# The first tile's expert rows finished inside the second tail, and VectorE's routing cut into six pieces

## What is computed

```
q = (h @ w_q).reshape(B, S, PEER_HEADS, 2, PEER_HALF)
s1, s2 = q against the two sets of 128 sub-keys
v1, i1 = top_k(s1, 16); v2, i2 = top_k(s2, 16)          # routing
top, ci = top_k(v1[:, None] + v2[None, :], 16)
expert = i1[ci // 16] * 128 + i2[ci % 16]; gate = softmax(top)
act = gelu(h . expert_down[expert]) * gate
y   = sum over the 128 experts of act * expert_up[expert]
```

## Time and profile before

| | |
|---|---|
| median of 3 runs| 4313.49 us (4313.34 to 4319.21)|
| the profiled execution| 4317.19 us, span 4315.4 us|
| PE busy| 2814.7 us (65%)|
| DVE busy| 2301.3 us (53%)|
| POOL busy| 1443.1 us (33%)|
| ACT busy| 541.6 us (13%)|
| data moved| 1413.21 MB|

### The profile page before, as it was taken

How to read it: one execution, slowest core, us unless ns; L and a number is a source line. 1 busy time by engine, 2 the same in 40 slices (tenths; PEclk the granted TensorE clock), 3 DMA queues, 4 the chain that set the end, 5 groups by cost and what they waited for, 6 DMA issues and landing times.

```text
span 4315.4 us, 37435 instructions
## 1 busy us (share of the span) xinstructions
PE 2814.7 (65%) x15012; PEld 1619.7 (38%) x15012; DVE 2301.3 (53%) x3585; ACT 541.6 (13%) x1191; POOL 1443.1 (33%) x1109
## 2 busy tenths in 40 slices
PE   3797899977899999997893334434344334434435
PEld 2686787877875555453451101101001001101101
DVE  7397697652176233325465555664555664444442
ACT  2211211210110000111111101100001001000000
POOL 2321212000003223233233356454356454354352
PEclk9898999988999999998995555555555555555555
DMA  7544424488658889889688899999999999999998
GB/s 287 183 173 149 139 99 163 171 328 316 201 198 342 305 347 367 344 336 366 253 322 335 355 404 422 412 413 422 416 399 412 412 412 422 421 422 422 421 421 370
DMA packets 303724, 1413.21 MB, mean 327 GB/s; under 512 B 24384, under 2 KB 24512, under 8 KB 167104
## 3 DMA queue, kind: packets, MB, share of 16 engines
q0 software_dynamic: 152064, 1107.36, 62.6%
q1 hardware_dynamic: 145568, 291.53, 19.4%
q10 hardware_dynamic: 5920, 11.94, 0.7%
HBM read 1403.35 MB, written 7.39 MB: 327 GB/s over the span
## 4 chain that ended last, share of the span: by engine, by line
PE 42%; DMA 37%; DVE 11%; POOL 5%; issue 4%; ACT 2%; SPq 0%; ACTq 0%; DVEq 0%; POOLq 0%
PE psum L610 42%; DMA front<-in_down,back 22%; DMA front<-in_up,back 9%; POOL front L581 4%; DVE front L1577 3%; DMA front<-in_w_in 2%; DMA back<-in_ada_w 2%; DVE back L1290 1%; DVE back L1352 1%; DMA back<-in_up,back 1%; ACT back L1116 1%; DVE back L1555 0%; POOL back L581 0%; DVE back L1512 0%; DVE back L1521 0%
## 5 line engine op out<-in xcount | busy, mean ns | idle before, releaser
L610 PE MATMUL psum<-front 128*32 128x512 f32 (+2 forms) x6608 | 1410.0, 664 | 999.2 <-DMA front<-in_up,back 851.8
L1577 DVE CUSTOM_DVE_ANT_0 front<-front,back 128x2048 f32<-128x2048 f32 x512 | 1168.7, 2291 | 1391.5 <-DMA front<-in_down,back 1274.4
L610 PEld LDWEIGHTS psum<-front 128*32 128x32 f32 (+1 forms) x6608 | 582.3, 163 | 1759.7 <-issue 1404.6
L581 POOL DMA_INDIRECT front<-in_down,back x512 | 622.1, 1215 | 930.1 <-DVE back L1577 657.6
L581 POOL DMA_INDIRECT front<-in_up,back x442 | 539.5, 1221 | 1001.1 <-PE psum L610 953.8
L610 PE MATMUL psum<-back,front 128*32 128x128 f32 (+3 forms) x4400 | 636.0, 457 | 331.9 <-DMA back<-in_up,back 164.2
L610 PEld LDWEIGHTS psum<-back,front 128*32 128x32 f32 (+1 forms) x4400 | 372.2, 168 | 603.1 <-issue 316.6
L559 POOL TENSOR_TENSOR w_low<-front,w_high 128x2048 fp32r<-128x2048 f32 x33 | 153.4, 4650 | 589.5 <-ACT w_high L1004 589.5
L610 PE MATMUL psum<-x_high,w_high 128*128 128x512 f32 x640 | 258.6, 404 | 51.1 <-issue 22.4
L610 PE MATMUL psum<-x_low,w_high 128*128 128x512 f32 x640 | 256.1, 400 | 0.0
L610 PE MATMUL psum<-x_high,w_low 128*128 128x512 f32 x640 | 255.9, 400 | 0.0
(11 more groups left out here) (160 smaller groups left out, 1700.5 us busy)
## 6 DMA issues: line engine op xcount, KB each, us to landing
front<-in_w_in SPq DMA_DIRECT2D x116, 1024.0 KB, 6.7
back<-in_ada_w SPq DMA_DIRECT2D x64, 1024.0 KB, 8.5
front<-in_ada_w POOLq DMA_DIRECT2D x32, 1024.0 KB, 8.6
front<-in_w_out SPq DMA_DIRECT2D x32, 1024.0 KB, 5.6
front<-in_w_q SPq DMA_DIRECT2D x32, 1024.0 KB, 5.4
front<-in_w_conv_o SPq DMA_DIRECT2D x16, 1024.0 KB, 6.8
front<-in_w_attn_o SPq DMA_DIRECT2D x16, 512.0 KB, 3.8
front<-in_down,back POOLq DMA_INDIRECT x512
```

Source lines behind the costliest of these rows:

```text
L581: nc.gpsimd.indirect_dma_start(out=row_, out_offset=None, in_=table[:, :], in_offset=bass.IndirectOffsetOnAxis(ap=idx4[:, t % 2, c:c + 1], ...
L610: return nc.tensor.matmul(o, a, b, start=start, stop=stop)
L1577: V.tensor_tensor_reduce(d_row[s], d_row[s], h2r, 1.0, 0.0, ALU.mult, ALU.add, pre[:, b // 16 % 2, b % 16:b % 16 + 1]).then_inc(dots_done, 1)
```

## The change

1. **Places instead of positions.** A new constant `DRAIN = 32` and `place(p)` split the walk in two. Positions 0 to 159 are the first tile alone: 128 blocks and 32 positions in which its lagging work (up rows, gelu, the last group's norm) drains. Positions from 160 on are blocks 128 to 511 as before, so block 128 begins at position 160. Everything that looks back (`b - LAG`, the unit, the group) only looks back inside its own part.
2. **A new pace.** `PACE[i] = min((i + 1) * 160 // 71, 160)`: 2.25 positions per chunk, in steps of 2, 2, 2, 3, and 160 is reached after chunk 71 (the end of the first `q` group). The chunks 72 to 83 have no retrieval work.
3. **GpSimd's order** follows: downs 0 to 127 with ups 0 to 105 in between, then ups 106 to 127 alone, then downs 128 to 149 alone, then pairs again.
4. **Routing in pieces.** `top16` is split into `first8` and `next8`, and `route(t, n)` into six steps. For tiles 2 and 3 the steps stand at every second position from 28 on, with two dot products between; `gates` moves to 20 positions after the first step, ScalarE's `gate_exp` from offset 34 to 44. In the tails all six steps still come in one go.
5. Two waits (`h2_quarter` for J = 4, `z_sum` for J = 3) name the counts that fit the new order.

```diff
-END = BLOCKS + 64
+DRAIN = 32
+END = BLOCKS + DRAIN + 64
+def place(p):
+    return (p, 0, 128) if p < 128 + DRAIN else (p - DRAIN, 128, BLOCKS)
 def block_pace():
-    at, out = 0, []
-    for i in range(tail_chunks(1)):
-        if 64 <= i < 67:
-            at += (3, 3, 2)[i - 64]
-        else:
-            at += 1 + i % 2
-        out.append(at)
-    assert at == 128, at
-    return out
+    last = 48 + 16 + TAIL[1][1] // P + 4
+    return [min((i + 1) * (128 + DRAIN) // last, 128 + DRAIN) for i in range(tail_chunks(1))]
...
-            for i in range(BLOCKS + UP_LAG):
-                if i < BLOCKS:
+            for first, last in ((0, 128), (128, BLOCKS)):
+                for i in range(first, last + UP_LAG):
+                    if i < last:
...
-                b = i - UP_LAG
-                if b >= 0:
+                    b = i - UP_LAG
+                    if b >= first:
...
                 if J >= 2 and i == 0:
-                    pe.wait_ge(out_ready, J - 1)
+                    pe.wait_ge(out_ready, J if J == 4 else J - 1)
...
-                pe.wait_ge(h2r_ready, min(4 * (J + 2), 4 * GROUPS))
+                pe.wait_ge(h2r_ready, 4 * (J + 1) if J in (3, GROUPS - 1) else 4 * (J + 2))
...
-                    p = pos_
-                    if p % 32 == 0 and p < BLOCKS:
+                    b, first, last = place(pos_)
+                    if b % 32 == 0 and b < last:
                         for i in range(4):
-                            h2_quarter(p // 32, i)
-                    if 0 <= p - LAG < BLOCKS:
-                        weighted_rows(p - LAG)
+                            h2_quarter(b // 32, i)
+                    if first <= b - LAG < last:
+                        weighted_rows(b - LAG)
...
-            def route(t, n):
+            def route(t, n, step):
...
-                    t, n = p // 128 + 1, (p % 128 - 28) // 24
-                    if 2 <= t < TT and p % 128 >= 28 and n < 4:
-                        if (p % 128 - 28) % 24 == 0:
-                            route(t, n)
-                        if (p % 128 - 28) % 24 == 12:
+                    t, n = b // 128 + 1, (b % 128 - 28) // 24
+                    if first and t < TT and b % 128 >= 28 and n < 4:
+                        step = (b % 128 - 28) % 24
+                        if step % 2 == 0 and step < 12:
+                            route(t, n, step // 2)
+                        if step == 20:
                             gates(t, n)
```

More of the change, by code:

```diff
@@ L586, in _ @@
             pool.wait_ge(ada2_used, 2 * KT)
-            for i in range(BLOCKS + UP_LAG):
-                if i < BLOCKS:
[L589 to L596, removed]
-                b = i - UP_LAG
-                if b >= 0:
[L599 to L604, removed]
+            for first, last in ((0, 128), (128, BLOCKS)):
+                for i in range(first, last + UP_LAG):
+                    if i < last:
+                        s, _, prev = D_SLOT[i]
+                        if i % 128 < 32 and i % 8 == 0:
+                            pool.wait_ge(routed, 4 * (i // 128) + i % 128 // 8 + 1)
+                        if prev is not None:
+                            pool.wait_ge(dots_done, prev + 1)
+                        if i == WIDE:
+                            pool.wait_ge(g_done, DONE[1, "sc", 3] + 4)
+                        gather(down, d_row[s], i, d_in[s])
+                    b = i - UP_LAG
+                    if b >= first:
+                        s, _, prev = U_SLOT[b]
+                        if prev is not None:
+                            pool.wait_ge(u_used, prev + 1)
+                        if b == WIDE:
+                            pool.wait_ge(g_done, DONE[1, "sc", 3] + 4)
+                        gather(up, u_row[s], b, u_in[s])
         @block.tensor
@@ L1144, in retrieve @@
                 while pos_ < upto:
[L1145 to L1155, removed]
+                    b, first, last = place(pos_)
+                    if b % 32 == 0 and b < last:
+                        h2_quarters(b // 32)
+                    unit = b // 16 - 1
+                    if first <= 16 * unit < last:
+                        if b % 16 == 3:
+                            unit_gelu(unit)
+                        if 7 <= b % 16 < 15:
+                            block_weights(16 * unit + 2 * (b % 16 - 7))
+                            block_weights(16 * unit + 2 * (b % 16 - 7) + 1)
+                    J = b // 32 - 1
+                    if first <= 32 * J < last and b % 32 == 24:
                         z_squares(J)
-                    if 0 <= J < GROUPS and p % 32 == 26:
+                    if first <= 32 * J < last and b % 32 == 26:
                         z_std(J)
-                    t, n = p // 128 + 1, (p % 128 - 34) // 24
-                    if t >= 2 and t < TT and p % 128 >= 34 and (p % 128 - 34) % 24 == 0 and n < 4:
+                    t, n = b // 128 + 1, (b % 128 - 44) // 24
+                    if first and t < TT and b % 128 >= 44 and (b % 128 - 44) % 24 == 0 and n < 4:
                         gate_exp(t, n)
@@ L1513, in top16, with next8 @@
                 st.seen(st.n)
+            def next8(vals, inds, src, count):
                 for i in range(count):
@@ L1605, in retrieve @@
                 while pos_ < upto:
[L1606 to L1608 removed]
+                    b, first, last = place(pos_)
+                    J = b // 32 - 1
+                    if first <= 32 * J < last and b % 32 == 28:
                         finish(J)
[L1610 to L1618 removed]
+                    if b < last:
+                        dot(b)
+                    unit = b // 16 - 1
+                    if b % 16 == 5 and first <= 16 * unit < last:
+                        unit_act(unit)
+                    t, n = b // 128 + 1, (b % 128 - 28) // 24
[4 more added lines that the diff above has]
+                        if step == 20:
                             gates(t, n)
@@ L1689, in tail @@
                     dve.wait_ge(act_took, ATOOK[c, "sc", i] + 4)
-                    route(c, i)
+                    for step in range(6):
+                        route(c, i, step)
                     if i:
```

76 lines of the change are left out of this document (38 added, 38 removed).

## The result

The changed kernel took 4361.27 us (median of 4, 4359.42 to 4366.44), the kernel before 4314.50 us in the same measurement: a ratio of 1.0111, 95% interval 1.0099 to 1.0124. The change costs 47 us. The forecast was 4300 us, with 4345 as the upper end of the range. The profiled span is 4357.6 us; my sum was 4302.

What follows compares the result with a forecast made beforehand. TensorE was taken to bound tail 1 and DMA the rest. 2364 + 65 + 1794 + 10 + 69 = 4302 us of span (tail +71, fewer pairs -44, routing -40, together -13), so 4300 us; range 4256 to 4345.

Steps and rivals of the forecast that it cites:

- Part 1: Beginning of tail 1: TensorE waits 21 us (17 to 24) for VectorE; the first twelve chunks end at 1386.
- Part 2: Dense stretch, chunks 13 to 57: DMA becomes the bound, 620 us; chunk 57 ends at 2007 (1965 to 2030).
- Part 3: End of tail 1: +5 us before the x chunks, -22 there, -21 in the q groups; block 128's dot at 2364.
- Part 4: After the tail, blocks 128 to 149, downs only: 22 x 2.97 = 65 us instead of 109 (2.485 to 3.46 each).
- Part 5: Routing of tile 2 onward: pieces fit into idle time, so 10 us of the 50 lost stay (3 to 50).
- The end: From the last dot to the end of the kernel: 69 us, as before.
- TensorE did not stay the bound: Rival for tail 1, chance 0.20: TensorE stays the bound, chunk 57 ends at 1965, time 4258 us.
- The clock: Rival for the dense stretch, chance 0.17: TensorE's waits put chunks at 1.2 GHz, 25.4 us each; with four, 4345 us.
- Collisions of gathers with pieces: Rival for the routing, chance 0.06: gather issues slow beside VectorE's pieces, up to 108 us, time up to 4408.
- Half the routing: Rival for the routing, chance 0.17: the pieces give back only half, since groups' beginnings empty the queue, 4320 us.

Runs made afterwards that it cites:

- e3: The changed kernel with PACE held at 13 for the first nine chunks, removing TensorE's wait at the w_attn_o product: 4354.75 us, 1.0091 of the kernel before.
- e9: The changed kernel with half of tail 1's gate products left out (less TensorE work, same loads): 4326.95 us, 1.0032 of the kernel before.
- e10: The changed kernel with only half of each gate weight chunk loaded in tail 1 (less DMA, same matmuls): 4334.05 us, 1.0051 of the kernel before.
- e6: The changed kernel without ScalarE's copy of h2r for groups 1 to 3: 4357.86 us, 1.0083 of the kernel before.
- e5: The changed kernel with five buffers from block 131 on instead of 160 (WIDE = 131): 4337.33 us, 1.0045 of the kernel before.
- e1: The kernel before with only the routing of tiles 2 and 3 in six pieces, no drain: 4290.23 us, 0.9938 of the kernel before.

## Why the prediction was wrong

The forecast was 13 us faster; the kernel is 47 slower. The forecast was a small difference of large terms, +71 against -84, and three of its terms were mis-sized in the same direction: 26 us up to block 128, 8 us in the stretch of down rows, 22 us behind it. Either of the two large ones alone turns the sign, since the forecast gain was 13 us. The order below is that of the prediction.

**Part 1 was right.** TensorE waits 23.3 us for VectorE (forecast 21, bounds 17 and 24), and the first twelve chunks end at 1383.6 (1386). e3 showed that taking the wait away brings 6.5 us and not 23: loads run during the wait, too, and would have to be made up behind it.

**Part 2 had the right mechanism and the wrong size; this is the largest step that failed.** DMA became the bound (share 0.99; e9, e10). Chunk 57 ended at 2035.3 and not at 2007, beyond my upper end of 2030. There were 258.0 MB in the stretch, 246 loads and not 242, some 10 us. Each took 2.52 us and not 2.56, which took 10 back. The rest is the 27 us of dips around the groups' beginnings. My upper end of 2030 stood for just that ("if each group's beginning, which stops the dots, also empties the queue"), and I took nothing of it into the value. The mixed stretch of 75 us in which DMA's share was 1.01 was a piece without a group's beginning, so it could not price one. Where the dips lie is shown; what makes them is open (e6).

**Part 3 was right.** From chunk 57 to the x chunks 93 us (92 to 93 by the forecast), the x stage 55.4 (77 - 22 = 55), the `q` groups 181.3 (184). The price of emptying them is what I saw and did not weigh: DMA idles at a share of 0.27 for 182 us. By DMA's price, the 22 up loads that moved are worth 22 x 2.485 = 55 us. The tail grew by 96.7, so 42 us were lost in it, where the forecast lost 16 (71 - 55).

**Part 4 was too low by 8 us:** 73.3 and not 65, 3.33 us per dot, inside the bounds of 2.485 and 3.46 and near the row from which the upper bound came. The nearest row was nearer than the middle that I took. e5 gives the cause, three buffers; with five it is 60.4, 2.74 us per dot.

**Part 5 was too low by 22 us:** 31.9 and not 10. The mechanism was right and its size half of the forecast: the pieces gave back 23 us in e1 (52.4 to 29.0) and 20.6 here, not 40. What stayed begins with the group at block 160: its dot waits 9.33 us for ScalarE as before (8.68), and some 8.5 us are lost there; I gave it 2. Some 3.5 more are lost from block 176 to 184, in the second routing, where the up blocks still have three buffers. Five buffers from block 131 on take 14.6 of the 31.9 us away, these two losses among them (e5). Some 17 us stay in every kernel with five, about 1.5 us for each of the 11 groups from block 160 to 480. The 42 us read from the slices were not all routing: slice 22 held this group too.

**The end:** 68.5 us (69).

**The rivals.** TensorE did not stay the bound: e9 gained 10 us in the stretch with TensorE's busy time 76 us lower.

The clock did fall, but for short times, and the rival's price did not come. Over the dense stretch the granted clock was 0.95 of 2.4 GHz, against 0.99 before. That mean hides two levels, here around 1515, where TensorE had waited 5.2 us for up rows, and in the 33 us behind:

```profile
1515.00:1521.00 6.00, 5.56 (x14) 2.41 (x15) 2.30 (x2) 0.00 (x0) 1.87 (x2) 0.50 1.02 415
1522.00:1555.00 33.00, 29.72 (x121) 14.38 (x119) 17.09 (x22) 0.22 (x1) 12.07 (x11) 1.00 1.02 415
```

0.95 between 1.2 and 2.4 GHz is a tenth of the 649 us, some 65 us, at 1.2 GHz. By this estimate at most half of that, 33 us, is work that TensorE lost, and it was idle for 66 of the 649 us. The longest piece at 1.2 GHz in the stretch is 10 us, shorter than one of the whole chunks of 25.4 us that the rival asked for. In e9 the clock was lower still, 0.87, and the way to chunk 57 was 10 us shorter, so the clock did not set the time. The page that I cited (the Trainium skill, TensorE: Matmul & The Clock Gate, HAM oscillation) tells of a kernel that falls back each round; the trace agrees that the clock falls at such waits: it did so 12 times between 1386 and 2035 us, each time at waits of 2 to 6 us.

The slower side was reached by another way than the rival that I had for it. Collisions of gathers with pieces did not show (423 GB/s with VectorE at 19.10 of 20 us). On the other page cited (the Trainium skill, GPSIMD Engine Reference, Specifications) the trace agrees that an issue can be slower beside a dot, 2.17 us in e5 against 0.93; at 2.47 us per load DMA was still full. "Half the routing" was near in size, 20.6 us given back and not 40, and its reason, the groups' beginnings, was in part the right one.

## What to carry to other kernels

Work moved from a stretch bound by one engine into a stretch bound by another is free only until the second one is full; count what the receiving stretch has room for, at the pace that the table sets, and look at what idles in the stretch left empty. Here 2.25 positions per chunk overfilled 45 chunks and emptied 12 (109 and 50 GB/s), and an even pace alone was worth 48 us. Price a stretch with few buffers by the row with few buffers, not by the steady one: three buffers gave 291 to 311 GB/s and five, after the first 10 us, 420. When a forecast is a small difference of large terms, its range is that of the terms added. The upper ends of my own parts 2, 4 and 5 (+23, +11, +40) reach a span of 4376 us, while the range that I stated ended at 4345. A blocking job of 18 us cut into pieces that fit between waits gained 25 us, and it was worth more than the rearrangement that it came with. An experiment that leaves something out should be read at the place where it acts before its result is: e6's dots still waited.

## What the runs showed of the hardware

- Gathers and weight loads together reach 413 to 418 GB/s, 2.52 us per load of 1 MiB, nearly the 421 to 423 of gathers alone. In the dense stretch 202.2 loads were gathers and 43.4 weights. If a gather costs 2.485 us there as it does alone, the 622 us outside the dips leave (622 - 502)/43.4 = 2.76 us for a weight load, an estimate, and not the 2.94 that I took from the queue's share in the earlier trace rows.
- A gather issue on GpSimd is slow when it starts while a dot of two SBUF inputs runs. In the changed kernel 188 of the 1024 issues do; 184 of these take over 1.1 us, up to 3.0, and nearly all end 0.8 us after the dot. Of the 836 others 826 take 0.93 to 1.1 us, though 334 of them still overlap a dot that begins later. With five buffers DMA keeps 420 GB/s even when each issue takes 2.17 us (e5).
- TensorE's granted clock falls to 1.2 GHz for 3 to 10 us at waits of 2 to 6 us in a stretch that is otherwise at 2.4 GHz: over the dense stretch its mean is 0.95 with TensorE busy 583 of 649 us, and 0.87 over 614 us with half of the gate products left out (471.9 us busy, e9), which is a quarter of the time at 1.2 GHz.
